# A hybrid encoder layer on one core: the middle pairs of the time mixing as a loop on TensorE, roots by logarithm, identity terms as whole matmuls

## The reference

```python
def _rwkv7_step(S, inp):
    r, w, k, v, a, b = inp
    Sa = jnp.einsum('zbhvk,zbhk->zbhv', S, a)
    S = S * w[..., None, :] + Sa[..., :, None] * b[..., None, :] + v[..., :, None] * k[..., None, :]
    return S, jnp.einsum('zbhvk,zbhk->zbhv', S, r)
...
kk = kk / jnp.maximum(jnp.sqrt(jnp.sum(kk * kk, axis=-1, keepdims=True)), 1e-12)
...
yn = ((y - mu) * lax.rsqrt(var + GN_EPS)).reshape(B, T, C) * ln_g + ln_b
```

## Time and profile before

| | us |
|---|---|
| median of three runs | 1827.98 (1826.15 to 1830.1) |
| the profiled execution, its own time | 1829.13 |
| its span, first to last instruction | 1827.3 |
| pairs of the time mixing, about 372 to 603 | 231 |
| TensorE busy in them | 200.3 |
| VectorE busy in them | 179.0 |
| ScalarE busy in them | 147.8 |

### The profile page before, as it was taken

The page is one execution under the profiler, slowest core; times in us unless marked ns, Lnnn a source line. Parts: engine busy times, 40 slices in busy tenths (PEclk is TensorE's granted clock), DMA queues, the critical chain, the costliest instruction groups (busy, mean ns, idle before and its releaser), DMA issues.

```text
span 1827.3 us, 37340 instructions
## 1 busy us (share of the span) xinstructions
PE 1716.3 (94%) x16231; PEld 1096.9 (60%) x16231; DVE 586.4 (32%) x1302; ACT 353.9 (19%) x945; POOL 63.1 (3%) x97
## 2 busy tenths in 40 slices
PE   8999999988989999999899999999999999999997
PEld 7887888867777445676545545454544444544443
DVE  2001333578886201022132322313132222222234
ACT  2122222267665201023100000000000000000002
POOL 1000000000000000002000000000000000000000
PEclk9999999999999999999999999999999999999999
DMA  9933353200000844328799999999999999999993
GB/s 308 206 110 101 110 165 138 92 4 4 4 4 5 297 164 177 130 113 301 291 426 430 429 429 430 431 432 427 433 428 433 428 433 427 433 428 430 429 419 148
DMA packets 95843, 503.65 MB, mean 276 GB/s; under 512 B 37869, under 2 KB 42369, under 8 KB 76913
## 3 DMA queue, kind: packets, MB, share of 16 engines
q1 hardware_dynamic: 90872, 488.17, 66.6%
q0 software_dynamic: 4608, 13.08, 2.4%
q10 hardware_dynamic: 248, 0.65, 0.1%
HBM read 511.29 MB, written 4.23 MB: 282 GB/s over the span
## 4 chain that ended last, share of the span: by engine, by line
PE 69%; DMA 22%; DVE 6%; issue 2%; ACT 1%; DVEq 0%; POOL 0%; SPq 0%; POOLq 0%; ACTq 0%
PE ps L1550 14%; PE ps L2067 8%; PE ps L2191 8%; PE ps L2056 8%; DMA ring<-in_wd 7%; DMA ring<-in_wu 7%; DMA rest<-in_wu 7%; PE ps L1874 6%; PE ps L2075 4%; PE ps L1892 2%; PE ps L1943 2%; PE ps L1960 2%; PE ps L1901 2%; PE ps L2047 1%; PE ps L1763 1%
## 5 line engine op out<-in xcount | busy, mean ns | idle before, releaser
L1550 PE MATMUL ps<-wide,ring 128*128 128x256 f32 x1248 | 275.3, 379 | 1.2 <-PE ps L1550 0.9
L1550 PEld LDWEIGHTS ps<-wide,ring 128*128 128x128 f32 x1248 | 239.0, 195 | 39.7 <-issue 10.1
L1410 DVE TENSOR_TENSOR tokA<-tokA,ps 128x512 f32<-128x512 f32 x256 | 158.5, 681 | 100.5 <-PE ps L2075 100.5
L2067 PE MATMUL ps<-ring,wide 128*64 128x256 f32 x1512 | 172.6, 387 | 16.8 <-DMA ring<-in_wu 16.6
L2191 PE MATMUL ps<-ring,gg 128*64 128x512 f32 x768 | 175.4, 598 | 2.3 <-DMA ring<-in_wd 1.6
L2056 PE MATMUL ps<-ring,wide 128*64 128x256 f32 x1536 | 173.0, 383 | 2.4 <-DVE wide L1398 2.4
L1423 DVE SCALAR_TENSOR_TENSOR gg<-ps,tmp,gg 128x256 f32<-128x256 f32 x32 | 15.5, 484 | 477.5 <-PE ps L2067 477.5
L2067 PEld LDWEIGHTS ps<-ring,wide 128*64 128x64 f32 x1512 | 110.5, 140 | 76.7 <-DMA ring<-in_wu 21.8
L2056 PEld LDWEIGHTS ps<-ring,wide 128*64 128x64 f32 x1536 | 109.8, 138 | 56.8 <-DVE wide L1398 4.0
L2075 PE MATMUL ps<-wide,gg 64*128 64x512 f32 x512 | 135.3, 627 | 0.9 <-ACT wide L824 0.8
L2191 PEld LDWEIGHTS ps<-ring,gg 128*64 128x64 f32 x768 | 50.9, 136 | 120.7 <-issue 111.9
(11 more groups left out here) (376 smaller groups left out, 2064.5 us busy)
## 6 DMA issues: line engine op xcount, KB each, us to landing
ring<-in_wg SPq DMA_DIRECT2D x23, 4096.0 KB, 28.6
ring<-in_wu SPq DMA_DIRECT2D x23, 4096.0 KB, 31.0
ring<-in_wd SPq DMA_DIRECT2D x22, 4096.0 KB, 32.0
rest<-in_wd SPq DMA_DIRECT2D x8, 4096.0 KB, 30.5
ring<-in_w_in SPq DMA_DIRECT2D x7, 4096.0 KB, 15.5
rest<-in_wu SPq DMA_DIRECT2D x7, 4096.0 KB, 29.7
rest<-in_wg SPq DMA_DIRECT2D x7, 4096.0 KB, 29.6
ring<-in_w_out SPq DMA_DIRECT2D x4, 4096.0 KB, 17.4
```

Source lines behind the costliest of these rows:

```text
L1410: V.tensor_tensor(fin_part(t, h, n), fin_part(t, h, n), ps[:, banks[q][h], :], ALU.add).then_inc(S["added"], 1)
L1550: ins = mm(ps[0:rows_, m % 2, 0:T], lhs, hnT[:, k, :], start=k == 0, stop=k == KD - 1)
L2067: ins = mm(ps[CAP * h:CAP * h + CAP, 1, 0:T], xT[:, k, CAP * i:CAP * i + CAP], w[:, T * h:T * h + T], start=k == 0, stop=k == KD - 1)
```

## The change

Three things are changed together.

First, TensorE's pairs 1 to 6 become a loop `Fori(1, CT - 1)`, whose waits compare with a register (`ready`). For that the pair's values are copied by GpSimd to a fixed place `VP` ahead of each pair. Some waits fall away (`rw_y0e`, `rw_dsq`, `rw_prep` and `rw_sq` but for the first pair), since another wait covers them.

Second, all inverse square roots are made on ScalarE as exp(-0.5 ln x), with one table that holds both functions, loaded by hand. VectorE's reciprocals and the table loads in the pairs go. VectorE's order in a pair changes: the next pair's key products of both directions now stand ahead of L1151, and `keys` moves ahead of the last two additions.

Third, the old sum in a solve's step is added by two matmuls over all 128 partitions, in place of four of 64x64. Besides, 36 matmuls of one column (`TINY`) run before the input has landed.

```diff
-                    for e, r, q, o in tiles():
-                        ins = mm(ps[o, 2 * g + e, CH:P], ident[q, q], src[q, g, e, 1, :], start=False, stop=True)
+                    for e in range(2):
+                        same_or_other = cst[:, ID + CH * e:ID + CH * e + P]
+                        ins = mm(ps[:, 2 * g + e, CH:P], same_or_other, src[:, g, e, 1, :], start=False, stop=True)
...
+            def ready(name, value):
+                pe.wait_ge(S[name], value)
+                if not isinstance(value, int):
+                    pe.sem_inc(S["pe_step"], 1)
...
-            for p in range(CT):
-                pair_(p, p == 0, p == CT - 1)
+            pair_(0, True, False)
+            with pe.Fori(1, CT - 1) as p:
+                pair_(p, False, False)
+            pair_(CT - 1, False, True)
...
 # GpSimd
             for n in range(4 * CT):
+                p, g = n // 4, n % 4
+                if g == 0:
+                    if p:
+                        pool.wait_ge(S["rw_kv"], 2 * p)
+                    pool.tensor_copy(VP, Vtok[:, :, P * p:P * p + P]).then_inc(S["rw_r1"], 1)
...
 # ScalarE
             def key_norm(p):
                 act.wait_ge(S["rw_n2e"], p + 1)
-                A(ew[:, SQ], ew[:, SQ], ACT.Sqrt).then_inc(S["rw_nrm"], 1)
+                A(ew[:, SQ], ew[:, SQ], ACT.Ln).then_inc(S["rw_nrm"], 1)
+                act.wait_ge(S["rw_nrm"], 2 * p + 1)
+                A(ew[:, SQ], ew[:, SQ], ACT.Exp, scale=-0.5).then_inc(S["rw_nrm"], 1)
...
 # VectorE, in pair_
+                if not last:
+                    key_norms(p + 1)
+                    unit_keys()
+                    products_ar(p + 1, 0)
+                    products_bk(p + 1, 0)
+                    products_out(0)
                 if not first:
                     inverse_std(p - 1)
                     normed_head(p - 1)
-                if not last:
-                    key_norms(p + 1)
-                if not first:
                     gated(p - 1)
                 dc.add(V.tensor_copy(BNS, ew[:, BON]))
                 if not last:
-                    unit_keys()
                     bonus_terms(p + 1)
-                    products_ar(p + 1, 0)
-                    products_bk(p + 1, 0)
-                    products_out(0)
+                    products_ar(p + 1, 1)
+                    products_bk(p + 1, 1)
+                    products_out(1)
...
+            pe.wait_ge(S["zeroed"], 2)
+            for _ in range(TINY):
+                mm(ps[0:32, 6, 0:1], idle[:, 0:32], idle[:, 0:1], start=True, stop=True)
```

More of the change, by code:

```diff
@@ L616, in exponential @@
                     act.wait_ge(S["rw_gnow"], p)
-                if n == 4 and not now:
+                if n == 0 and not now:
                     act.wait_ge(S["rw_prep"], p)
@@ L665, in pair_ @@
                 if not last:
-                    A(warm, warm, ACT.Sqrt)
+                    key_norm(p + 1)
                 for g in range(4):
@@ L678, in pair_ @@
                     A(PRN[(l + 1) % 2][:, g, :, k], got[:, :, k], ACT.Copy).then_inc(S["rw_pte"], 1)
-                    if n == 9:
-                        if not first:
-                            head_std(p - 1)
-                        if not last:
-                            key_norm(p + 1)
+                    if n == 9 and not first:
+                        head_std(p - 1)
                 for g in range(4):
@@ L697, in pair_ @@
                 if next_:
-                    for n in range(3, 8):
+                    for n in range(8):
                         exponential(p + 2, n)
@@ L825, in job @@
                     if last:
-                        A(warm, warm, ACT.Sqrt)
+                        log_and_exp()
                         for k, (n, t, h) in enumerate(FIN[0:4]):
@@ L842, in _, with last_std @@
                 job(NE // 2 - 1, 1, last=True)
+            def last_std(t):
+                one = slice(t, t + 1)
+                act.wait_ge(S["row_sum"], t + 2)
+                A(stat(5, 2)[:, one], stat(5, 0)[:, one], ACT.Ln, scale=1.0 / D, bias=eps).then_inc(S["ln_done"], 1)
+                act.wait_ge(S["ln_done"], 7 + t)
+                A(stat(5, 2)[:, one], stat(5, 2)[:, one], ACT.Exp, scale=-0.5).then_inc(S["std_done"], 1)
             for i, (n, t, h) in enumerate(FIN):
@@ L1159, in pair_ @@
                 V.tensor_copy(Yp.rearrange("p (c t) -> p c t", c=NCH), ps[:, 0:4, T:T + CH]).then_inc(S["rw_y0e"], 1)
-                if not last:
-                    dve.wait_ge(S["rw_gnow"], p + 2)
-                    products_ar(p + 1, 1)
-                    products_bk(p + 1, 1)
-                    products_out(1)
+                if next_:
+                    keys(p + 2)
                 dc.sync()
@@ L1680, in half_of @@
                 return slice(CH * c, CH * c + CH)
+            def ready(name, value):
+                pe.wait_ge(S[name], value)
+                if not isinstance(value, int):
+                    pe.sem_inc(S["pe_step"], 1)
             def pair_(p, first, last):
-                pe.wait_ge(S["rw_prep"], p + 1)
+                if first:
+                    ready("rw_prep", p + 1)
                 for g in range(4):
@@ L1692, in pair_ @@
                         pe.wait_ge(S["v_ev"], 4)
-                    if g == 0 and not first:
-                        pe.wait_ge(S["rw_y0e"], p)
                     if g == 2 and not first:
-                        pe.wait_ge(S["rw_yp"], p)
+                        ready("rw_yp", p)
                     for i, keys_ in enumerate((BT, KT)):
@@ L1706, in pair_ @@
                 if not last:
-                    pe.wait_ge(S["rw_sq"], p + 2)
+                    if first:
+                        ready("rw_sq", p + 2)
                     ins = mm(ps[:, 7, T:2 * T], ones2, ew[:, SQ], start=True, stop=True)
@@ L1805, in pair_ @@
                     ins.then_inc(S["rw_y0"], 1)
-                pe.wait_ge(S["rw_tte"], 4 * p + 4)
+                ready("rw_tte", 4 * p + 4)
                 def chunk(i, z):
@@ L1842, in pair_ @@
                 inputs(0)
-                pe.wait_ge(S["rw_y0e"], p + 1)
+                ready("rw_y0e", p + 1)
                 inputs(1)
```

156 lines of the change are left out of this document (68 added, 88 removed).

## The result

The changed kernel takes 1898.2 us (median of four runs, 1897.1 to 1899.7), the kernel before 1827.2 on the same chip: 3.8% slower, ratio 1.0382 (95% interval 1.0367 to 1.0397). I had said 1897.

The account below looks back on a forecast made before the run. TensorE, busy 94% of the span, was taken as the bound, setting the pace in the solve. 8 x (12.6 - 4.2) = +67.2, loop +2.4, start and end -1.3: +68.3 on 1829.1, forecast 1897 us, range 1875 to 1915.

Parts of the forecast that it names:

- (d): Solve: the identity as two whole matmuls adds 0.65 us a step (bounds 0.30 and 0.75), 12.6 us a pair.
- the first and the second rival: Solve's identity: first, change of form hidden, 1844 us, chance 0.17; second, whole matmuls cost no more than tiles, 1796 us, 0.12.
- (a): Solve: TensorE's idle time waiting for instructions goes away, a gain of 2.8 us a pair.
- (b): Behind the solve: VectorE, without its reciprocals, is no longer late, a gain of 1.4 us a pair.
- (e): Pair loop: registers and `pe_step` increments cost 0.4 us a pair (bounds 0 and 1.0), 2.4 us for six pairs.
- Start and end: Outside the pairs: faster warm-up matmuls gain 0.6 us at the start, the final norm 0.7 at the end, together -1.3.
- The third rival: Pair loop: its code is fetched again each turn, 2.8 us idle stays in six pairs, jumps cost 2: 1926 us, chance 0.06.

Follow-up runs that it names:

- e4: The changed kernel with TensorE's eight pairs written out in place of the loop, whole identity and new roots kept: 1892.5 us.
- e8: The changed kernel with TensorE's pairs written out and two more whole matmuls in every solve step, into unread columns: 1964.2 us in one run.
- e2: The kernel before with only the identity changed, to two whole matmuls; old roots, no loop: 1895.2 us.
- e5: The changed kernel with the identity as four 64x64 tiles again and TensorE's pairs written out, new roots kept: 1823.4 us.

## Why the prediction was right, step by step

**(d), the identity: right in mechanism and size.** I had 1.10 us for a step (0.45 + 0.65), the chain shows 1.09. L1769 cost 0.80 with the change of form behind it; now it adds 0.49, as that change is in the step's 1.09 already: 0.31 less, where I had 0.37. So (d) is 20 x 0.64 - 0.31 = 12.5 us, against 12.6. With the 8.5 us that the prediction had for a solve without idle time that makes 21.0; e4's solve takes 20.92. e8 shows 0.11 us for each of the trace's matmuls of this form, as the earlier trace rows had it; the first and the second rival fall with the chain itself. That it is the loads that take this time was not tried apart: it is argued from the same weights with 256 columns, which take 0.21, so that 64 columns alone would be 0.05. The step grew by 0.64; less the four matmuls' 0.45, and with the tiles' own 0.12 back, 0.31 are left for the two changes of form, where I had 0.37. Of the two rules from "TensorEngine Tiling (Array Packing)" in the Trainium skill, the one in Key Properties (the array drains when the form changes) agrees with these 0.31 us; the other, Instruction Overhead, would have a matmul at some 60 cycles, an estimated 0.025 us at 2.4 GHz and about a quarter of the 0.11 us measured.

**(a) and (b): right in sum, wrong in cause.** The whole identity alone has a period of 37.29 us: 8.39 more than before, so 4.1 of the 12.5 came back, 2.9 in the solve as (a) and 1.2 behind it as (b), where I had 2.8 and 1.4. All of it is there because the solve is slower, nothing through the loop or the roots. For (a) I had named the slower solve for pairs 0 and 7 only; for (b) I had named it as a help to the missing reciprocals, and it does without them. In this the prediction was lucky: two parts of the change that it counted as gains give nothing in these pairs, and the part that it counted as a cost alone brings them.

**(e), the loop's registers: mis-sized.** I put 0.4 us a pair, at most 1.0; it is 38.55 - 37.29 = 1.26, six times 7.6 us in place of 2.4 (the whole runs are 5.7 us apart). Where I looked for it, at the copies of the states, it is: L1831 waits 0.4 us, twice a pair, where with the pairs written out the trace lists no wait of TensorE at all between 406 and 640 us. A register is worked out between L1820 and L1831. The timeline of the change:

```profile
524.97 0.33 PE L1831 MATMUL ps<-ring 64*64 64x64 f32 x4 [0.46 <-PE ps L1820]
...
526.33 0.33 PE L1831 MATMUL ps<-ring 64*64 64x64 f32 x4 [0.41 <-PE ps L1820]
...
527.83 1.98 PE L1700 MATMUL ps<-ring 64*64 64x128 f32 x64 [0.16 <-issue]
```

The jump itself costs 0.16, as good as nothing, when the body is in place. With the jump the two waits make 1.03 of the 1.26 us. That the releaser is TensorE's own line fits register work; the registers alone were not tried.

**Start and end: too small to be read from one trace.** I had -0.6 at the start, from warm-ups that the 36 small matmuls would speed. The change's trace has them at 4.42 us, against 4.61:

```profile
1.72 4.00 PE L1488 MATMUL ps<-gg 128*32 128x1 f32 x72 [1.72 <-POOL tmp L452]
7.90 4.42 PE L1491 MATMUL ps<-gg 128*128 128x256 f32 x10 [2.18 <-DMA tokA<-in_x]
```

But the same ten take 4.07 us in e2, which has no small ones, and 4.63 in e5, which has all 36:

```profile
8.19 4.07 PE L1498 MATMUL ps<-gg 128*128 128x256 f32 x10 [8.19 <-DMA tokA<-in_x]
```

```profile
7.69 4.63 PE L1491 MATMUL ps<-gg 128*128 128x256 f32 x10 [1.97 <-DMA tokA<-in_x]
```

Over all traces it is 4.07 to 4.61 us without them and 3.91 to 4.64 with them, so no effect is seen. Whole stretches scatter likewise. The first addition of pair 0 comes at 375.7 to 377.0 us in the three kernels with the old roots and at 374.0 to 376.2 in the eleven with the new; what lies behind the stage takes 1223.2 to 1225.7 us with the old roots, and 1221.8 to 1225.3 with the new where the experts' loop stays. By the means that is -1.7 and -0.9, together -2.6 in place of my -1.3, and the +0.4 and -3.9 of the change's own trace lie at the edges of it. So (e) was 5.2 us too small, and start and end gave 1.3 to 2.2 more than I had. These errors offset each other in part, and the hit is a little better than its working.

**The third rival, the loop's code doesn't stay, had the wrong condition.** I gave it 0.06, since the experts' loop is "as long". That one has 1,601 instructions by the count of the table, this one 1,783, and by the rule above it fits by 6. Had the program ahead of it been 36 small matmuls shorter, the time would have been 1936.7, above my range, and above the rival's own 1926: a jump costs 4.4 us where I had 2, and behind it the granted clock is at half, while the 2.8 us of idle time that the rival kept in each pair are not there (0.5 us of waits for instructions in the whole stage, besides the jumps). Of a begin position taken at random only 10 in 256 keep this body in place, by the rule. That this one is among them was luck: twelve instructions fewer ahead of the loop (33 small matmuls) upset it.

## What to carry to other kernels

Before code is put into a loop for the fetch's sake, ask whether it was the fetch that cost: here a slower solve hid it anyway, and the loop cost 1.26 us a pair, most of it at waits next to register work. A loop near the size that stays in place must be measured with its begin shifted by some instructions, or its body made at least 255 instructions shorter than the room, which by the rule above is 1,537 or less, so that edits far ahead of it can't undo it. The experts' loop is over that, and an edit in the pairs undid it at a price of 18 us. And before four small tiles are merged into whole matmuls for fewer instructions, price the weight loads and both changes of form on the chain that sets the pace.

## What the runs showed of the hardware that was not expected

- A TensorE loop of 1,783 instructions runs its second to sixth round without one instruction packet if it begins 3 or 7 instructions behind a boundary of 256, takes 9 packets every second round at 19, and 9 every round at 116, 243 and 247. From best to worst that is 1898.2 to 1947.1 us, with the same work in the loop. The experts' loop of 1,601 has no packet with begins from 5 to 149 (one in a single trace) and 9 a jump at 254.
- A jump to code that isn't there costs 4.3 to 5.1 us idle in the kernels without small matmuls and with 40, and where the target's packet holds only about the first 8 instructions, 3.36 and a second wait of 2.39. In the experts, with the DMA engines busy at a mean share of 0.95, it costs 11.6 to 12.0.
- Behind a wait of 4.35 us at a jump the granted clock is 0.50 for the first 3.6 us, so 64 matmuls take 3.69 us in place of 1.98. In the kernel with tiles in the loop the clock is 0.81 over a whole period.
- One kernel's ten warm-up matmuls take 3.91 to 4.64 us from trace to trace, and the stages ahead of and behind the pairs differ by 2 to 4 us where the code is the same, so a term of 1 us there needs more than one trace.
